# Moving the copy of the attention output on ScalarE, its square, and two tap updates on VectorE

## The reference

```
a = softmax(q k^T / 8)                    # 4 heads, 2 maps each, 512 x 768 keys
w = a[:, :, 0] - lam * a[:, :, 1]
o = w @ v                                 # per head, 128 wide
attn = rmsnorm(o, subln) * (1 - lam_init)
u = short_conv(proj_hy)                   # 3 taps over time, 12 tiles of 128 channels
v, x1, x2 = split(u);  z = long_conv and gates;  hyo = rmsnorm(z)
x = x + g_a * (concat([attn, hyo]) @ w_out)
```

## Time and profile before

| | |
|---|---|
| median of three runs | 1725.31 us |
| the profiled execution | 1726.43 us, its span 1724.6 us |
| mean granted TensorE clock | 0.988 |
| PE busy | 1669.1 us (97%) |
| DVE busy | 973.9 us (56%) |
| ACT busy | 693.9 us (40%) |
| chain that ended last, by engine | PE 82%, DVE 8%, ACT 4%, DMA 2% |
| steps 6 to 17 of the attention | from 239.3 to about 320 us |

### The profile page before, as it was taken

The page is one execution under the profiler, slowest core; times in us unless marked ns, Lnnn a source line. Parts: engine busy times, 40 slices in busy tenths (PEclk is TensorE's granted clock), DMA queues, the critical chain, the costliest instruction groups (busy, mean ns, idle before and its releaser), DMA issues.

```text
span 1724.6 us, 18861 instructions
## 1 busy us (share of the span) xinstructions
PE 1669.1 (97%) x7232; PEld 1283.0 (74%) x7232; DVE 973.9 (56%) x1350; ACT 693.9 (40%) x1040; POOL 135.2 (8%) x144
## 2 busy tenths in 40 slices
PE   6999999989999999999999999999999999999997
PEld 2478765457788888888788787567876888888885
DVE  5757587575544434435789597665534373535352
ACT  4431355413443223325654667955433331212131
POOL 0202000122300000004000000312000100000001
PEclk9899999999999999999999999999999999999999
DMA  9434124502133233323142021425211222222221
GB/s 310 161 116 157 64 62 144 186 1 98 51 98 97 91 104 98 97 90 130 50 170 93 18 74 53 140 86 195 98 50 49 98 98 98 98 98 97 97 97 49
DMA packets 113560, 175.07 MB, mean 102 GB/s; under 512 B 3979, under 2 KB 56779, under 8 KB 112972
## 3 DMA queue, kind: packets, MB, share of 16 engines
q1 hardware_dynamic: 109724, 161.33, 27.6%
q0 software_dynamic: 3760, 12.72, 2.3%
HBM read 169.58 MB, written 4.46 MB: 101 GB/s over the span
## 4 chain that ended last, share of the span: by engine, by line
PE 82%; DVE 8%; ACT 4%; DMA 2%; issue 2%; SPq 1%; DVEq 0%; ACTq 0%
PE bank L870 16%; PE bank L872 16%; PE bank L871 16%; PE bank L907 6%; PE bank L908 6%; PE bank L912 5%; PE bank L1146 2%; PE bank L1008 2%; PE bank L1161 1%; DMA weight_slots<-in_w_mod 1%; PE bank L1088 1%; PE bank L1100 1%; DVE weight_slots_lo L2303 1%; PE bank L1291 1%; PE bank L1488 1%
## 5 line engine op out<-in xcount | busy, mean ns | idle before, releaser
L3155 POOL TENSOR_TENSOR arena<-arena 128x512 f32<-128x512 f32 (+1 forms) x50 | 70.2, 1410 | 972.8 <-ACT arena L1593 969.5
L872 PE MATMUL bank<-hx_hi,weight_slots_lo 128*128 128x512 f32 x320 | 124.8, 390 | 0.0
L3110 DVE TENSOR_TENSOR weight_slots_lo<-weight_slots,weights_hi 128x2048 fp32r<-128x2048 f32 x30 | 67.4, 2288 | 98.1 <-ACT weights_hi L2262 98.1
L1562 ACT ACTIVATE weights_hi<-weight_slots 128x2048 fp32r<-128x2048 f32 (+2 forms) x46 | 77.2, 1722 | 109.3 <-DMA weight_slots<-in_ffn_w_down 58.2
L2262 ACT ACTIVATE weights_hi<-weight_slots 128x2048 fp32r<-128x2048 f32 x30 | 55.8, 1909 | 161.7 <-DMA weight_slots<-in_w_up 114.6
L871 PE MATMUL bank<-xn_lo,weights_hi 128*128 128x512 f32 x288 | 112.1, 389 | 0.0
L1548 ACT ACTIVATE arena<-bank 128x512 f32<-128x512 f32 (+2 forms) x110 | 54.9, 538 | 115.9 <-PE bank L872 50.6
L870 PE MATMUL bank<-sq_hi,weights_hi 128*128 128x512 f32 x256 | 99.6, 389 | 0.0
L871 PE MATMUL bank<-sq_lo,weights_hi 128*128 128x512 f32 x256 | 99.6, 389 | 0.0
L872 PE MATMUL bank<-sq_hi,weight_slots_lo 128*128 128x512 f32 x256 | 99.6, 389 | 0.0
L1593 ACT ACTIVATE arena<-arena 128x512 f32<-128x512 f32 (+1 forms) x80 | 46.1, 586 | 104.8 <-DVE arena L3129 28.4
(11 more groups left out here) (431 smaller groups left out, 4106.4 us busy)
## 6 DMA issues: line engine op xcount, KB each, us to landing
weight_slots<-in_w_in SPq DMA_DIRECT2D x24, 1024.0 KB, 7.3
weight_slots<-in_ffn_w_up SPq DMA_DIRECT2D x22, 1024.0 KB, 6.8
weight_slots<-in_w_up SPq DMA_DIRECT2D x16, 1024.0 KB, 6.6
weight_slots<-in_w_down SPq DMA_DIRECT2D x16, 1024.0 KB, 6.8
weight_slots<-in_w_mod SPq DMA_DIRECT2D x14, 1024.0 KB, 8.4
arena<-in_w_mod POOLq DMA_DIRECT2D x32, 256.0 KB, 3.4
weight_slots<-in_w_out SPq DMA_DIRECT2D x8, 1024.0 KB, 8.6
weight_slots<-in_w_xkv SPq DMA_DIRECT2D x8, 1024.0 KB, 7.4
```

The lines of the kernel that those rows point to most:

```text
L872: return mm(ps, ll, rh, start=False, stop=stop)
L1562: A(high_half(kind, n, i), W[:, s_, a:b], ACT.Copy).then_inc(w_hi, 1)
L3110: V.tensor_tensor(W_lo[:, s % 2, a:b], W[:, s % 2, a:b], W_hi[:, s % 2, a:b].bitcast(F32), ALU.subtract).then_inc(w_lo, 1)
L3155: G.tensor_tensor(acc, acc, sq[i % 2][:, 0:width], ALU.add).then_inc(sq_added, 1)
```

## The change

Three edits, all in the attention steps. PE's list of instructions stays as it is.

1. ACT: the copy of o_h to `obuf` leaves its place between the exponentials of map 1 and of map 0, and comes at the end of steps 6, 10 and 14, behind the weight copies, the Hyena split and the modulation row.
2. ACT: the square of `obuf` leaves the end of those steps. It comes one step later, directly ahead of the 1/rms, behind that step's `hyena_mid` or modulation row (`output_norm`, line 1751, which was used for the last head alone).
3. DVE: in steps 7 and 11 `hyena_taps` came ahead of `score_max`; now it comes behind it, as in all other steps.

```diff
@@ -1730,8 +1730,6 @@
                     act.wait_ge(sem("w_ready"), n - 1)
                 st = stat[:, n % 2, :]
                 for m in (1, 0):
-                    if m == 0 and n in O_STEPS:
-                        output_copied(O_STEPS[n])
                     if m == 0 and n >= 2:
 
                         done(act, f"wt_{(n - 2) // NT}_{(n - 2) % NT}_1")
@@ -1769,17 +1767,16 @@
                     attention_exp(n)
                 if 2 <= n < HEADS * NT + 2:
                     weights_out(*divmod(n - 2, NT))
-                if n in O_STEPS:
-                    evicted(act, f"o_{O_STEPS[n]}")
-                    norm_squares(f"norm_o_{O_STEPS[n]}", lambda k: obuf)
                 for columns_ in HY_SPLITS.get(n, ()):
                     split_hyena(*columns_)
                 if n in HY_STEPS:
                     hyena_mid(HY_STEPS[n])
                 if n in STEP_MOD:
                     mod_rows_out(STEP_MOD[n])
+                if n in O_STEPS:
+                    output_copied(O_STEPS[n])
                 if n in NORM_O_STEPS:
-                    norm_factor(f"norm_o_{NORM_O_STEPS[n]}", L, 2 * DH)
+                    output_norm(NORM_O_STEPS[n])
 
             for o in range(2):
                 for t in range(NT):
@@ -2518,11 +2515,9 @@
             score_max(0)
             for n in range(HEADS * NT):
 
-                if n in HY_STEPS and n in NORM_O_STEPS:
-                    hyena_taps(HY_STEPS[n])
                 if n + 1 < HEADS * NT:
                     score_max(n + 1)
-                if n in HY_STEPS and n not in NORM_O_STEPS:
+                if n in HY_STEPS:
                     hyena_taps(HY_STEPS[n])
                 combine(*divmod(n, NT))
                 for columns_ in HY_SPLITS.get(n, ()):
```

## The result

The changed kernel takes 1738.26 us (median of four runs, 1736.79 to 1739.73), the kernel before 1725.87 beside it: a ratio of 1.0074, 95% interval [1.0055, 1.0091]. That is 12.4 us or 0.7% slower. The forecast was 1737.5. The profiled execution took 1738.75 us with a span of 1736.9, against 1726.43 and 1724.6. Its mean granted TensorE clock is 0.988, as before.

The account below looks back on a forecast made before the run. PE bounds steps 6 to 8, DVE's softmax from step 12, the slab transfer the attention's end. 9.2 us at full clock plus 2.8 for the clock makes 12.0: 1737.5 us, own range 1735 to 1740, eight in ten 1731.5 to 1741.

Parts of the forecast that it names:

- Copy late, 1.5 + 0.5: Steps 6 and 10: PE stalls 1.5 us within wt_1_1, then 0.5 us, for the bank the late copy empties.
- The rival in which eight banks hide it: Bank rotation makes late copy and taps free; 4.6 us left, 6.3 with one clock fall, 1731.6 us; chance 0.10.
- Square late, 1.4 twice: Steps 7 and 11: PE stalls 1.4 us before norm_o_0 and again before norm_o_1, waiting for the square.
- Taps late, 2.6: Before hy_9 in step 8: PE waits 2.6 us for the bank that DVE's second tap of hy_8 frees.
- Step 12, 0.95 more: Taps between score_max and combine delay step 12's softmax chain by 0.95 us beyond the 1.9 us from PE.
- Step 15, 0.8: Late square delays norm_o_2; the slab transfer's cover is used up, leaving 0.8 us at the attention's end.
- The sum at full clock, 9.2: All waits in the attention steps without clock falls: 1.5 + 1.4 + 2.6 + 2.85 + 0.8 = 9.2 us.
- The clock, 2.8: PE's clock may halve after the gaps ahead of hy_9 and norm_o_2; 2.8 us taken for both together.
- a third gap, in step 12, has cover: The gap ahead of step 13's scores costs nothing, as PE has 1.5 us to spare in these 12 us.
- I see no place that gives it back: After 324 us everything starts by its predecessors, so none of the 12.0 us loss is recovered.
- The freed ACT: Rival: second exponential pair starts sooner, softmax gains 2.8 us in each of three steps; 1726.1 us; chance 0.05.
- No slower than before: The other side, same rival: 8.4 us gained cancels all but 0.8 of the 9.2; chance 0.05.

Follow-up runs that it names:

- changed kernel filled everywhere: Changed kernel with unread matmuls in PE's long waits, both in the attention steps and at five places further on: 1731.43 us, ratio 1.0035 to the kernel before.
- the other filled kernel: Kernel before with unread matmuls at five of PE's idle places outside the attention steps: 1721.31 us, ratio 0.9975 to the kernel before.

## Why the prediction came out right, point by point

*Copy late, 1.5 + 0.5.* Right in mechanism and place: a stall within wt_1_1 that the copy behind the split ends, and a smaller one in step 10 (0.42 of idle, 0.5 predicted). The edit alone shows it. The rival in which eight banks hide it is out: the bank rotation that the Trainium skill recommends ("Perfetto Trace Analysis", "Optimizing Tensor Performance") is in place here, and a reader eight short jobs back still stalled PE, 1.37 us of idle.

*Square late, 1.4 twice.* Right: 1.48 us of idle, twice. *Taps late, 2.6.* Right: the idle is 2.69, and it goes when the tile has another bank. *Step 12, 0.95 more.* Right, 0.92. *Step 15, 0.8.* Right, 0.76; mod_11 has no wait for its slab, the cover was used up.

*The sum at full clock, 9.2.* It is 10.3. The term mis-sized is the restart, which I had at nothing. Up to the scores of step 12 the table has 8.6 against 7.4, over five waits some 0.2 us each. The waits' idle times alone (1.37, 1.48, 2.69, 0.42 and 1.48) make 7.44. Two rows of the kernel before show most of the rest, for norm_o_0:

```profile
254.36 0.39 PE L872 MATMUL bank<-hx_hi,weight_slots_lo 128*128 128x512 f32 x1
254.59 1.02 PE L843 MATMUL bank<-arena,ones 128*128 128x512 f32 x2
```

In a running stream a row starts 0.16 us before the last one ends (254.36 + 0.39 - 254.59). Behind a wait that overlap is lost, and the norm sum takes 1.10 us and not 1.02.

*The clock, 2.8.* Here the two profiles of the changed kernel differ. In the attention of the first the falls cost 4.9 us: 1.58 behind hy_9's wait (7.81 - 6.23), 1.70 in o_2, and 1.6 between norm_o_2 and mod_11 (15.16 - 12.78 - 0.76). The step that failed is "a third gap, in step 12, has cover": there and with edit 3 alone the clock fell not at the gap but some us later, in o_2, which nothing covers. And "I see no place that gives it back" was wrong, as 2.2 us came back where the kernel before has falls as well, which were shorter after the shift. 4.9 - 2.2 = 2.7: in this execution two errors cancel. In the second profile both steps hold: the falls that count are behind hy_9 and behind norm_o_2, the one in step 12 is covered, nothing comes back, and the clock costs 13.7 - 10.3 = 3.4 us. So the mechanism of this term is right in one execution and the size right by luck in the other.

*The freed ACT.* Out, by ACT's row at 246.13. "No slower than before" is out by the interval, [1.0055, 1.0091].

Still open: why a fall follows a wait in one profile and not in another. One of 1.61 us was followed by a fall, one of 3.13 wasn't, and the expectation above that an idle time of 2 us brings it on did not hold. That the fall in o_2 belongs to the wait of 2.60 us in step 12 is argued, not shown: it came in two of the three profiles with that wait, and in none of those without it. Filling the waits takes most falls away; in the changed kernel filled everywhere one was left, at 1326 us, where the other filled kernel had none.

## What to carry to other kernels

Before an instruction that empties a bank is moved later, look up how soon the bank's next user comes, in time and not in number of jobs: eight short jobs were 2.7 us here. A new wait on PE cost here the wait, plus some 0.2 us to start again, plus, where the clock fell on work that was waited for, another 1.4 to 1.7 us, at the wait or one stage later. Where PE must wait a few microseconds, matmuls that nobody reads, into a bank that is free anyway, were worth 4 us here twice.

## What the runs showed that I had not expected

The same wait of 2.62 us left the clock up in one kernel (first matmul 0.50 us) and down in another (0.80, granted 0.57). A fall need not stand at the wait: in the changed kernel PE had idled 2.60 us from 299.25, ran at full clock from 304 to 308, and o_2 from 310.78 took 1.70 us longer. Three edits cost 4.8, 7.1 and 8.3 us one by one by the medians and 12.4 together, while their waits at full clock, read place by place, add up (10.26 and 10.26). The total times of single runs could not be added up here; the shifts read from the profiles could.
